# Stick-breaking attention in five steps per head pair, with values two steps later, in a hybrid attention block

## What is computed

```
h = x @ w_in + b_in;  q_a,k_a,v_a,gate_a, q_b,k_b,v_b,gate_b, mg_a,mg_b = split(h)
# A: window attention, chunks of 64, each sees 2 chunks, 8 heads, sinks in the softmax
# B: stick-breaking, 8 heads, blocks of 128 queries:
z = q_b k_b^T * D**-0.5
log_keep = where(key < query, -softplus(z), 0)
between = reversed_cumsum(log_keep) - log_keep
w = where(key < query, exp(log_sigmoid(z) + between), 0);  o_b = w v_b
sub = (sigmoid(mg_a) * (o_a*silu(gate_a)) @ w_up_a + sigmoid(mg_b) * (o_b*silu(gate_b)) @ w_up_b) @ w_out
out = layer_norm(2**0.25 * x + sub)
```

## Time and profile before

| | |
|---|---|
| median of three runs | 754.43 us |
| the profiled execution | 754.92 us |
| its span, first to last instruction | 753.2 us |
| PE busy | 98% of the span |
| DVE, ACT, POOL busy | 69%, 54%, 15% |

### The profile page before, as it was taken

One profiled execution on the slowest core, in us unless ns is written; L12 is line 12 of the kernel. 1 busy time (PEld: TensorE's weight loads), 2 busy tenths in 40 slices (PEclk: granted clock), 3 DMA queues, 4 the chain that ended last, 5 costly groups with the idle time before them and its releaser, 6 DMA issues.

```text
span 753.2 us, 10645 instructions
## 1 busy us (share of the span) xinstructions
PE 738.4 (98%) x3940; PEld 579.0 (77%) x3940; DVE 518.1 (69%) x759; ACT 405.9 (54%) x760; POOL 109.3 (15%) x130
## 2 busy tenths in 40 slices
PE   9999989999999999999999999999999999999996
PEld 7888867776777777777777778888877888888884
DVE  6997878764897868768786974455584565570654
ACT  6954467675766666666676765555573122150321
POOL 0000000001232222223232210000000000000792
PEclk9999999999999999999999999999999999999999
DMA  8245322221101021020103123455536433350351
GB/s 308 84 98 125 113 71 85 70 60 52 57 2 57 15 71 37 21 85 0 57 1 98 55 73 114 139 188 191 192 134 245 168 113 139 112 205 19 132 192 69
DMA packets 41204, 76.22 MB, mean 101 GB/s; under 512 B 12224, under 2 KB 16320, under 8 KB 41152
## 3 DMA queue, kind: packets, MB, share of 16 engines
q1 hardware_dynamic: 41152, 75.54, 30.6%
HBM read 55.07 MB, written 18.35 MB: 97 GB/s over the span
## 4 chain that ended last, share of the span: by engine, by line
PE 90%; DVE 5%; ACT 3%; issue 1%; POOL 0%; ACTq 0%; DVEq 0%; POOLq 0%
PE ps L184 24%; PE ps L186 24%; PE ps L185 23%; PE ps L1513 5%; PE ps L1542 5%; PE ps L1529 4%; PE ps L1473 1%; PE ps L1446 1%; PE ps L1463 1%; PE ps L1358 1%; ACT beta_big L937 1%; DVE x_lo L1111 1%; DVE t_ops L1111 1%; ACT keep_big L935 1%; ACT prob L897 1%
## 5 line engine op out<-in xcount | busy, mean ns | idle before, releaser
L184 PE MATMUL ps<-x_hi,w_hi 128*128 128x512 f32 x416 | 168.7, 405 | 0.5 <-DVE w_lo L1268 0.3
L186 PE MATMUL ps<-x_hi,w_lo 128*128 128x512 f32 x416 | 162.6, 391 | 0.0
L185 PE MATMUL ps<-x_lo,w_hi 128*128 128x512 f32 x416 | 162.2, 390 | 0.0
L184 PE MATMUL ps<-t_ops,w_hi 128*128 128x512 f32 x304 | 123.5, 406 | 0.3 <-DVE w_lo L1092 0.3
L186 PE MATMUL ps<-t_ops,w_lo 128*128 128x512 f32 x304 | 119.2, 392 | 0.0
L185 PE MATMUL ps<-t_ops,w_hi 128*128 128x512 f32 x304 | 118.9, 391 | 0.0
L1092 DVE TENSOR_TENSOR w_lo<-raw,w_hi 128x512 fp32r<-128x512 f32 x120 | 81.8, 697 | 44.6 <-ACT w_hi L678 44.6
L184 PEld LDWEIGHTS ps<-x_hi,w_hi 128*128 128x128 f32 x416 | 78.1, 188 | 27.9 <-issue 11.6
L186 PEld LDWEIGHTS ps<-x_hi,w_lo 128*128 128x128 f32 x416 | 78.1, 188 | 17.0
L185 PEld LDWEIGHTS ps<-x_lo,w_hi 128*128 128x128 f32 x416 | 78.3, 188 | 14.2
L1224 DVE TENSOR_TENSOR_SCAN keep_big<-keep_big 128x1023 f32<-128x1023 f32 (+3 forms) x32 | 63.4, 1980 | 36.0 <-POOL keep_big L623 34.0
(11 more groups left out here) (182 smaller groups left out, 1214.3 us busy)
## 6 DMA issues: line engine op xcount, KB each, us to landing
raw<-in_w SPq DMA_DIRECT2D x28, 512.0 KB, 4.3
raw<-in_w SPq DMA_DIRECT2D x44, 256.0 KB, 2.9
sig_d<-sig_m SPq DMA_DIRECT2D x32, 256.0 KB, 3.7
sig_m<-sig_d SPq DMA_DIRECT2D x16, 512.0 KB, 4.2
xr<-in_xt SPq DMA_DIRECT2D x16, 256.0 KB, 6.8
raw<-in_xn SPq DMA_DIRECT2D x8, 512.0 KB, 3.7
out<-o_t SPq DMA_DIRECT2D x16, 256.0 KB, 2.3
o_t<-o_d SPq DMA_DIRECT2D x7, 512.0 KB, 5.1
```

The lines of the kernel that those rows point to most:

```text
L184: pe.matmul(out, w_hi, x_hi, start=first, stop=False, skip_group_check=goes_on)
L185: pe.matmul(out, w_hi, x_lo, start=False, stop=False, skip_group_check=goes_on)
L186: return pe.matmul(out, w_lo, x_hi, start=False, stop=last, skip_group_check=goes_on)
```

## The change

**Steps.** A pair of heads takes five steps in place of four (`PER_PAIR = 5`), and a step is one set of eight key blocks in one set of buffers, with one or two query tiles in it (`parts`): tile 0 with 8 blocks; tiles 1 and 7 (7 + 1); 2 and 6 (6 + 2); 3 and 5 (5 + 3); tile 4 with 4 blocks. The blocks to be computed stay 36 per pair. The four buffers become `keep0`, `keep1` (in turn by step) and one `beta`.

**Products.** They are whole again and no longer cut: three in a step, two in the last of a pair (`made`), 14 per pair as before, up to product 98 (`STEP_END`).

**Order of a step s.** PE: values of step s - 2, scores of s, turning of s - 1 (blocks 0 to 3), product, turning of s - 1 (blocks 4 to 7), the other products. ACT: keep of s, copies of turned blocks of s - 1, reading and rounding of the first product between and behind them, and beta of s only when all blocks of s - 1 are turned. DVE: gating of s - 2, the scans of head 0, `after` of the first product, the scans of head 1, `after` of the second, the weighting, `after` of the third. POOL cuts each tile's diagonal: as many cuts as before in all.

**Window attention.** In DVE's loop, for chunks 1 to 4 the maxima (now `row_maxima`) stand ahead of `prob_norm` of the chunk before.

```diff
-STEPS = 4 * PAIRS
+PER_PAIR = 5
+STEPS = PER_PAIR * PAIRS
+def parts(s):
+    j = s % PER_PAIR
+    if j in (0, PER_PAIR - 1):
+        return [(j, 0, 8 - j)]
+    return [(j, 0, 8 - j), (8 - j, 8 - j, j)]
+def made(s):
+    at = STEP_0 + 2 * NP * (s // PER_PAIR) + 3 * (s % PER_PAIR)
+    return range(at, at + (2 if s % PER_PAIR == PER_PAIR - 1 else 3))
...
-    for s in range(STEPS + 1):
-        if s > 0:
-            order += [("t", 2 * (s - 1) + 1, g) for g in range(unit_banks(s - 1, True))]
-            order += [("o", 2 * (s - 1) + 1, 0)]
...
-        order += [("t", 2 * s, g) for g in range(unit_banks(s, False))]
-        order += [("o", 2 * s, 0)]
+    for s in range(STEPS + 2):
+        if s >= 2:
+            order += [("o", s - 2, 0)]
+        if 1 <= s <= STEPS:
+            order += [("t", s - 1, g) for g in range(step_banks(s - 1))]
+        if s < STEPS and s % PER_PAIR == 0:
+            order += [("v", s // PER_PAIR, g) for g in range(2)]
...
                 if i == MG_PAIR + 1:
...
                     if pos == 4:
-                        act.wait_ge(z_done, 2 * STEPS)
+                        act.wait_ge(z_done, STEPS)
...
             for s in range(STEPS):
-                betas(s, False)
...
+                made_here = made(s)
+                keeps(s)
                 if s > 0:
-                    turned_blocks(s - 1, True, (0, 1))
...
+                    turned_blocks(s - 1, (0, 1))
+                read_bank(made_here[0])
+                if s > 0:
+                    turned_blocks(s - 1, (2, 3))
+                split_next(made_here[0])
+                betas(s)
+                after(made_here[1])
...
             for c in range(NCHUNK + 4):
-                if 1 <= c <= NCHUNK:
+
+                if 1 <= c <= 4:
+                    row_maxima(c)
                     prob_norm(c - 1)
...
             for s in range(STEPS):
-                break_sticks(s, False)
-                if s > 0:
-                    gated_out(s - 1, True)
...
+                made_here = made(s)
+                if s >= 2:
+                    gated_out(s - 2)
+                break_sticks(s, 0)
+                after(made_here[0])
+                break_sticks(s, 1)
+                after(made_here[1])
+                weigh(s)
+                if s % PER_PAIR == 0:
+                    gate_b_product(s // PER_PAIR)
+                for q in made_here[2:]:
+                    after(q)
...
             for s in range(STEPS):
-                scores(s, False)
...
+                made_here = made(s)
+                if s >= 2:
+                    values(s - 2)
+                scores(s)
                 if s > 0:
-                    turn(s - 1, True, (0, 1))
-                fill(s, 1)
+                    turn(s - 1, (0, 1))
                 if s > 0:
-                    values(s - 1, True)
+                    product(made_here[0])
...
+                if s > 0:
+                    turn(s - 1, (2, 3))
+                product(made_here[1])
```

More of the change, by code:

```diff
@@ L540, in _ @@
             for s in range(STEPS):
-                for place in range(5):
-                    for q in completed(s, place):
-                        after(q)
-                    if s % 4 == 0 and s > 0 and place == 2:
-                        p = s // 4 - 1
-                        sp.wait_ge(o_set, 8 * (p + 1))
+                for q in made(s):
+                    after(q)
+                    if s % PER_PAIR == 1 and s > 1 and q == made(s)[0]:
+                        p = s // PER_PAIR - 1
+                        sp.wait_ge(o_set, SB * (p + 1))
                         sp.dma_start(o_d[4 + p], o_b[p % 2][:]).then_inc(ob_out, 16)
-            for q in range(STEP_0 + NP * STEPS // 2, N_PRODUCTS):
+            for q in range(STEP_END, N_PRODUCTS):
                 if q in (LAST_PAIR + 1, LAST_PAIR + 2):
@@ L733, in room @@
                             if p >= 2:
[L734 removed]
+                                act.wait_ge(z_done, PER_PAIR * (p - 1))
                     if i == pair_vg(p):
@@ L1233, in gated_out, with weigh @@
-            def gated_out(s, small):
-                i = 2 * s + small
-                p, t = s // 4, unit(s, small)[0]
-                o = o_b[p % 2][:, P * t:P * (t + 1)]
-                dve.wait_ge(o_done, i + 1)
-                if s % 4 == 0:
+            def weigh(s):
+                dve.wait_ge(beta_cut, tiles_before(s + 1))
+                dve.wait_ge(scanned, 2 * tiles_before(s + 1))
+                for _, first, end in weight_pieces(s):
+                    dve.tensor_tensor(beta[:, :, first:end], beta[:, :, first:end],
+                                      keep[s % 2][:, :, first - 1:end - 1], ALU.mult).then_inc(w_ready, 1)
@@ L1240, in gated_out @@
+            def gated_out(s):
+                p = s // PER_PAIR
+                dve.wait_ge(o_done, s + 1)
+                if s % PER_PAIR == 0:
                     dve.wait_ge(gate_set, 2 * p + 2)
-                dve.tensor_tensor(o, o, ps[:, 6 + RING_AT["o", i, 0] % 2, 0:P], ALU.mult).then_inc(o_set, 1)
+                for i, (t, _, _) in enumerate(parts(s)):
+                    o = o_b[p % 2][:, P * t:P * (t + 1)]
+                    dve.tensor_tensor(o, o, ps[:, 6 + RING_AT["o", s, 0] % 2, P * i:P * (i + 1)],
+                                      ALU.mult).then_inc(o_set, 1)
```

329 lines of the change are left out of this document (142 added, 187 removed).

## The result

The changed kernel takes **763.8 us**, the median of four runs (762.9 to 764.8); the kernel before took 754.6 beside it. The ratio is 1.012, 95% interval 1.0105 to 1.0134: slower by 9.2 us, where I had forecast 12. The execution that was profiled took 762.90 with a span of 761.1; that of before 754.92 with 753.2. It is smaller than the 9.2 of the medians, since the profiled execution of the changed kernel was the fastest of its four.

What follows compares the result with a forecast made beforehand. PE, busy for 98% of the span, was taken as the bound. Terms -12.9 + 22.6 - 2.5 + 5.1 = +12.3 on the profiled 754.92 gave 767.2; predicted 767 us, range 752 to 778.

Steps and rivals of the forecast that it cites:

- part 1: PE, stick-breaking stage: fewer, longer runs save 3.05 us a pair, and a first-step wait of 0.66 goes; -12.9 us.
- part 2: DVE's chain through a step: gating frees the second turning bank late, so PE waits; +22.6 us.
- part 3: Window stage, chunk 3: with the maxima first, PE's wait shrinks and the clock's fall goes; -2.5 us.
- part 4: PE's clock: three falls behind the new waits, at most 1.7 us each; +5.1 us, bounds 0 and +17.
- The clock at every wait of about 2 us: Rival: PE's clock falls at each such wait, nine or ten falls, 17 us, not 5.1; 779 us; chance 0.15.
- The turning behind scores costs more: Rival, on PE: this or a product run of 24 costs 0.2 to 0.4 us at 20 places; 773 us; chance 0.13.
- DVE in time, in half or at all: Two rivals: half the waits or more go, 750.8 us, chance 0.12; DVE not late at all, 739.5, chance 0.08.
- The runs do not merge: Rival, on PE: the 4.0 us belong to other things, part 1 gives 1 a pair; 775 us; chance 0.04.
- no dip of the clock at 106: Sign in the window stage: no granted clock under 1.00 at 106 if right; still down there if wrong.

Runs made afterwards that it cites:

- experiment 1: Changed kernel with the gating of the step before put behind the weighting, ahead of the `after` of the last product: 741.86 us, ratio 0.9831.
- Experiment 9: Kernel before with only the window part of the change, the maxima first: 751.83 us, ratio 0.9963.
- experiment 5: Changed kernel with two small added DVE instructions of 128 columns straight ahead of each step's gating: 779.05 us, ratio 1.0333.
- Experiments 3 and 4: Each against the changed kernel: 3, ACT rounds before copying turned blocks 4 to 7, 758.05 us; 4, both heads' scans ahead of the first `after`, 756.29 us.
- experiment 6: Changed kernel with five small added DVE instructions of 128 columns straight ahead of each step's gating: 799.58 us, ratio 1.061.

## Why the prediction was right, and where its sizes were off

The sign, the place and the mechanism were right. The balance of the two spans against the sum of the prediction, in us:

```
                                            forecast    measured
part 1, fewer and longer runs on PE          -12.9       -11.8
part 2, waits for gating and weighting       +22.6       +21.4
part 3, the maxima first                      -2.5        -3.4
part 4, the clock in the stick stage          +5.1        +1.7
sum                                          +12.3        +7.9
```

- **Part 1, -11.8.** This is the stick-breaking stage of experiment 1 against that of the kernel before, from the start of the products ahead of the first scores to the end of the last values: 269.8 for 282.5 us, with 2.7 for one product more that is left behind the stage, and without its wait of 1.8 for the weighting. It also follows from the table: 2.97 in three pairs, 2.3 in the first, which had no waits for ACT, and the 0.66 of the earlier trace rows. That half of what 20 starts of products cost goes with half of them was a choice; it was 2.06 for my 2.0, but 0.3 of it is a wait, so a start that goes gives 0.17 to 0.18 and not 0.2. I had put the turning behind scores at nothing; it costs 0.06 to 0.12 us at a place, within my bounds. These misses of a few tenths a pair were nearly made good by the waits for ACT (the 0.7 a pair in experiment 1), which I had not counted: that the sum came within 1.1 us is in part luck.
- **Part 2, +21.4:** 19.7 of listed waits where I had forecast 22.6, and 1.7 that I had not forecast at all: it is what the stage takes more than in experiment 1 beyond the listed waits and the fall, 0.5 a pair (12.29 - 4.07 = 8.22 for 7.73 in the table), the price of stopping and starting again. So the waits were 2.9 too high and a cost was missing, and the sum is nearer than its parts. The count of DVE's chain held well. It said that DVE could take its first `low_part` 5.7 us after PE's restart, and it is 282.82 - 277.20 = 5.6. It said that the gating of a step of 6 and 2 ends 13.9 us in; it is 290.73 + 0.48 - 277.20 = 14.0. For 7 and 1 it said 15.8, and it is 276.77 + 0.28 - 261.39 = 15.7. The wait there was forecast as 2.0 and was 1.67, because PE itself comes back later than I counted: after 277.20 - 1.67 - 261.39 = 14.1, not 13.9. The 0.3 that I had added for sums through ACT did not all appear. In the last pair it was 3.49 for 3.9 and 1.78 for 1.9.
- **Part 3, -3.4:** the first product run of the stage begins at 174.7 for 178.1. The waits went from 2.63 to 0.38 and 0.58, so 1.67, and the fall of the clock, 1.3, went with them: 3.0. The other 0.4 is not explained; with the same code up to there, eight profiles reach this place at 174.6 to 175.8. I had expected 1.2 us of wait at the first output's copy, and it was 0.58. Experiment 9 confirms the 3.0 by itself (-2.9).
- **Part 4 is the step that was off.** "I take three falls" rested on one case in the trace, a wait of 2.63 with a fall and one of 0.66 without. The trace has one fall, behind the 3.49:

```profile
448.00:449.00 1.00, 0.23 (x2) 0.26 (x3) 1.00 (x4) 0.00 (x0) 0.00 (x0) 1.00 0.00 0
449.00:450.00 1.00, 1.00 (x7) 0.91 (x6) 0.76 (x1) 0.56 (x1) 0.00 (x0) 0.86 0.00 0
450.00:453.00 3.00, 3.00 (x8) 2.35 (x8) 0.00 (x0) 0.03 (x1) 0.00 (x0) 0.50 0.00 0
```

Seven waits of 1.67 to 1.73 us brought none. The fall costs half of 3.4 us. (The clock falls once more in the last microseconds of every kernel here, when PE has nothing left to do.) So of the 4.4 us between the forecast and the measured sum, 3.4 are two falls that did not come, 1.2 is part 2 and 0.9 part 3, against 1.1 that part 1 gave less. This is the balance of one execution: two of the four (764.3 and 764.8 us) have a mean granted clock of 0.993 for the 0.995 of the other two, as one more fall would make it, but none of these two was profiled. PE's busy time fell by 7.8 us, where the prediction said about 10.

The rivals. *The clock at every wait of about 2 us*: refuted here, one fall in the profile and not nine; but experiment 5 shows how near it was, since 0.5 us more of wait brought six more falls. The Trainium skill (TensorE: Matmul & The Clock Gate, A second HAM failure mode: psum-queue depth-cycling) says that short stops, often repeated, make the clock go back and forth: no trace here shows it at 1.7 us, and the trace of experiment 5 agrees at 2.2 to 2.3, with six falls at seven such stops. *The turning behind scores costs more*: true in kind, 0.06 to 0.12 us, under the 0.2 to 0.4 that it needed. *DVE in time, in half or at all*: refuted by the list of waits. Experiments 3 and 4 come part of the way to half the waits by the order of two lines, and experiment 1 reaches the kernel without them: the forecast of that case was 739.5, or 741.4 with the last turning's 1.9 of wait, and the kernel took 741.9. *The runs do not merge*: refuted by the table. The pair takes 70.08 us, where I had said 70 or more, and there is no dip of the clock at 106:

```profile
84.00:108.00 24.00, 23.55 (x132) 18.18 (x132) 20.93 (x44) 15.20 (x54) 0.00 (x0) 1.00 0.27 88
```

## What to carry to other kernels

When steps are made longer so that the bound engine changes its work less often, the gain is real only if the engine that frees its buffers still gets there within a step: count that chain instruction by instruction from the moment the buffer is taken, with the instructions queued ahead of the one that frees it. Here 11.8 us were won on PE and 21.4 lost in waits for DVE, and putting the freeing instruction ahead of work that was not yet needed gave back all but the last turning's 1.8. A loss of time like that is one of order, not of load: DVE was busy for 67% of the span, less than the 69% before.

## What the runs showed of the hardware

- The length of a stop of PE does not decide by itself whether the clock falls. In the twelve profiles of this study, leaving out the start and the last microseconds, it fell at no stop of under 2 us (45 of 1.0 to 1.8 us), during or behind six of seven of 2.19 to 2.33 (experiment 5), but behind one of four of 2.03 to 2.18 (experiment 6); behind 2.63 and not behind 2.58 at the same place; behind five of seven of 3.17 to 3.32 (experiment 6), three of four of 3.49, and both of 4.0 and 5.0. One that had no fall, from experiment 6, as a row of PE's timeline and then the stretch that it begins:

```profile
289.31 0.63 PE L1551 MATMUL ps<-ident,beta 128*128 128x128 f32 x4 [3.17 <-DVE o_b L1259]
```

```profile
289.00:293.00 4.00, 3.69 (x21) 3.15 (x22) 2.41 (x3) 0.85 (x2) 0.00 (x0) 1.00 0.00 0
```

- What decides between 2 and 3.5 us stays open. The moment differs too: 2.1 us into the stop in the earlier trace rows, but about 1 us after PE had started again in the changed kernel (448.77, and the 0.86 of 449 to 450). Where many such waits stand, the runs spread: 776 to 782 us in experiment 5, 797 to 804 in experiment 6, within 4 us in every other kernel.
- A stop of PE costs more than its listed length: a stopped turning takes 1.03 to 1.04 us without its wait, an undisturbed one 0.85 (the changed kernel and experiment 1).
- Ten runs of products fewer in a pair gave 2.06 us, of which 0.31 was a wait, so 0.17 to 0.18 each; five runs more, between scores and turning, cost 0.69, 0.14 each (the table of experiment 1).
